# Post-norm and residual add of two feed-forwards and two mixers, re-ordered by bank and token tile, with the last store split

## What is computed

```python
u = rms_norm(x, norm_gains[layer, 0])
mix = mixer(u, ...)                               # "mix0" / "mix1"
x = x + rms_norm(mix, norm_gains[layer, 1])
u = rms_norm(x, norm_gains[layer, 2])
ff = conv_ffn(u, w_up, conv_w, conv_b, w_down)    # D_FF = 2816
x = x + rms_norm(ff, norm_gains[layer, 3])        # layer 1: this is the output
```

## Time and profile before

| | us |
|---|---|
| median of 3 executions | 1035.88 (1035.08 to 1036.29) |
| the profiled execution, its own time | 1036.02 |
| span of its profile | 1034.6 |
| TensorE matmul busy | 981.4 (95%) |
| VectorE busy | 735.9 (71%) |
| ScalarE busy | 617.1 (60%) |
| POOL busy | 40.5 (4%) |

### The profile page before, as it was taken

How to read it: one execution, slowest core, us unless ns; L and a number is a source line. 1 busy time by engine, 2 the same in 40 slices (tenths; PEclk the granted TensorE clock), 3 DMA queues, 4 the chain that set the end, 5 groups by cost and what they waited for, 6 DMA issues and landing times.

```text
span 1034.6 us, 16633 instructions
## 1 busy us (share of the span) xinstructions
PE 981.4 (95%) x6732; PEld 838.1 (81%) x6732; DVE 735.9 (71%) x1137; ACT 617.1 (60%) x1001; POOL 40.5 (4%) x37
## 2 busy tenths in 40 slices
PE   6999989999999999998999999979999979999996
PEld 5877768987778998886888888879888868888885
DVE  4866465746576778676777777776976668777776
ACT  5655664436765764576656665675447666566655
POOL 0000000000000125000000000002200000000000
PEclk9999998999999999999999999999999989999999
DMA  8733344554235432325456666635544636666551
GB/s 293 240 99 119 102 143 122 183 171 135 82 102 164 135 110 85 121 82 182 145 192 192 186 184 187 192 112 162 165 125 130 195 107 201 187 194 187 183 183 41
DMA packets 43564, 158.34 MB, mean 153 GB/s; under 512 B 4960, under 2 KB 5344, under 8 KB 43360
## 3 DMA queue, kind: packets, MB, share of 16 engines
q1 hardware_dynamic: 42480, 154.00, 47.7%
q0 software_dynamic: 576, 2.10, 0.7%
q10 hardware_dynamic: 432, 1.20, 0.3%
HBM read 156.22 MB, written 1.05 MB: 152 GB/s over the span
## 4 chain that ended last, share of the span: by engine, by line
PE 73%; DVE 12%; ACT 11%; issue 2%; DMA 2%; ACTq 0%; DVEq 0%
PE psum L393 72%; DVE w_lo L379 4%; ACT w_hi L370 2%; DVE u_lo L559 1%; ACT u_hi L548 1%; PE psum L402 1%; DMA feat<-in_norm_gains 1%; DVE scr L2736 1%; ACT normed L491 1%; DMA const<-in_table 1%; ACT scr L2726 0%; ACT normed L2606 0%; DVE x_res L2873 0%; ACT L2361 0%; DVE scr L2864 0%
## 5 line engine op out<-in xcount | busy, mean ns | idle before, releaser
L379 DVE TENSOR_TENSOR w_lo<-raw,w_hi 128x1024 fp32r<-128x1024 f32 x288 | 351.8, 1225 | 136.9 <-ACT w_hi L370 136.8
L370 ACT ACTIVATE w_hi<-raw 128x1024 fp32r<-128x1024 f32 x288 | 302.7, 1056 | 205.3 <-PE psum L393 204.9
L393 PE MATMUL psum<-u_both,w_hi 128*128 128x512 f32 x704 | 250.3, 398 | 0.6 <-DVE u_both L559 0.6
L393 PE MATMUL psum<-u_both,w_lo 128*128 128x256 f32 x704 | 197.6, 281 | 0.0
L393 PE MATMUL psum<-w_hi,u_hi 128*128 128x512 f32 x432 | 176.6, 409 | 10.7 <-DVE u_lo L559 4.1
L393 PE MATMUL psum<-w_lo,u_hi 128*128 128x512 f32 x432 | 170.6, 395 | 0.0
L393 PE MATMUL psum<-w_hi,u_lo 128*128 128x512 f32 x432 | 170.5, 395 | 0.0
L393 PEld LDWEIGHTS psum<-u_both,w_hi 128*128 128x128 f32 x704 | 132.2, 188 | 33.2 <-DVE u_both L559 0.9
L393 PEld LDWEIGHTS psum<-u_both,w_lo 128*128 128x128 f32 x704 | 132.9, 189 | 1.5
L393 PE MATMUL psum<-u_hi,w_hi 128*128 128x256 f32 x384 | 111.0, 289 | 2.2 <-DVE w_lo L379 1.8
L393 PE MATMUL psum<-u_lo,w_hi 128*128 128x256 f32 x384 | 108.6, 283 | 0.0
(11 more groups left out here) (290 smaller groups left out, 1174.9 us busy)
## 6 DMA issues: line engine op xcount, KB each, us to landing
raw<-in_pieces SPq DMA_DIRECT2D x288, 512.0 KB, 3.7
feat<-in_norm_gains POOLq DMA_DIRECT2D x4, 512.0 KB, 5.2
const<-in_table SPq DMA_DIRECT2D x1, 1240.0 KB, 7.2
x_res<-in_x SPq DMA_DIRECT2D x1, 512.0 KB, 4.9
x_res<-in_x ACTq DMA_DIRECT2D x1, 512.0 KB, 5.1
out_x<-x_res SPq DMA_DIRECT2D x1, 512.0 KB, 2.7
out_x<-x_res ACTq DMA_DIRECT2D x1, 512.0 KB, 2.8
cols<-in_cols SPq DMA_DIRECT2D x1, 380.0 KB, 4.2
```

The lines of the kernel that those rows point to most:

```text
L370: act.q.activation(w_hi[i % SPLIT][:, :], raw[i % RAW][:, :], ACT.Copy).then_inc(act.done, act.mark("hi", i))
L379: dve.q.tensor_tensor(w_lo[i % SPLIT][:, :], raw[i % RAW][:, :], w_hi[i % SPLIT][:, :].bitcast(F32), ALU.subtract).then_inc(dve.done, dve. ...
L393: return pe.q.matmul(o, lhs, rhs, start=start, stop=stop, **kw)
```

## The change

At the mixers' ends VectorE does product and add of token tile 0, then product and add of token tile 1. At the feed-forwards' ends TensorE signals every bank; ScalarE squares the banks in order and makes the root of each token tile by itself; VectorE multiplies a bank after it has been squared, joins the sums by token tile, and adds by halves, token tile 0 before the last product of token tile 1, in both layers. After feed-forward 0 TensorE turns all of token tile 0 before token tile 1. The store of token tile 1 is made in two halves of columns, the first from ACT's queue, the second from SP's. The number of products, squares and transposes stays; there is one more sum, Ln and Exp to each feed-forward, two half adds in place of each full add in layer 1, and one more DMA.

```diff
         sp.wait_ge(dve, "f1", "x", 0)
         sp.q.dma_start(out[0, 0:P, :], x_res[:, 0, :]).then_inc(out_written, 16)
-        sp.q.wait_ge(out_written, 32)
+        sp.wait_ge(dve, "f1", "x", 1)
+        sp.q.dma_start(out[0, P:2 * P, NC:D], x_res[:, 1, NC:D]).then_inc(out_written, 16)
+        sp.q.wait_ge(out_written, 48)
...
         for t in range(ST):
             dve.wait_ge(act, "mix_sq", l, 1, t)
             dve_mix_gain(l, 1, t)
-        for t in range(ST):
             dve.wait_ge(act, "rstd", name, t)
             dve.wait_ge(dve, "mix_gain", l, 1, t)
             dve.q.scalar_tensor_tensor(x_res[:, t, :], mix_gained[:, t, :], post_rstd[name][:, t:t + 1], x_res[:, t, :],
...
-            if t == 0 and j == FT - 1:
-                last.then_inc(pe.done, pe.mark("ffn", l, 0))
+                if j == FT - 1 and (t, c) != (ST - 1, 1):
+                    last.then_inc(pe.done, pe.mark("ffn", l, t, c))
...
     def act_ffn_end(l):
...
+        act_ffn_square(l, 0, 0)
+        act_ffn_square(l, 0, 1)
+        act_ffn_square(l, 1, 0)
+        act_ffn_rstd(l, 0)
+        act_ffn_square(l, 1, 1)
+        act_ffn_rstd(l, 1)
+
+    def dve_ffn_gain(l, t, c):
+        cs = slice(c * NC, (c + 1) * NC)
+        dve.wait_ge(act, "square", f"f{l}", t, c)
+        dve.q.tensor_tensor(ffn_gained[:, t, cs], ffn_out[:, t, cs], post_gain[:, cs], ALU.mult).then_inc(
+            dve.done, dve.mark("times_gain", f"f{l}", t, c))
+
+    def dve_ffn_sum(l, t):
+        for c in range(2):
+            dve.wait_ge(act, "square", f"f{l}", t, c)
+        dve.q.tensor_tensor(post_sums[f"f{l}"][:, t:t + 1], ffn_sums[:, 0, t:t + 1], ffn_sums[:, 1, t:t + 1],
+                            ALU.add).then_inc(dve.done, dve.mark("post_sum", f"f{l}", t))
+
+    def dve_ffn_add(l, t):
+        dve.wait_ge(act, "rstd", f"f{l}", t)
+        for c in range(2):
+            cs = slice(c * NC, (c + 1) * NC)
+            dve.wait_ge(dve, "times_gain", f"f{l}", t, c)
+            dve.q.scalar_tensor_tensor(x_res[:, t, cs], ffn_gained[:, t, cs], post_rstd[f"f{l}"][:, t:t + 1],
+                                       x_res[:, t, cs], ALU.mult, ALU.add).then_inc(
+                dve.done, dve.mark(f"f{l}", "x" if c else "x0", t))
...
     def dve_ffn_end(l):
...
+        dve_ffn_gain(l, 0, 0)
+        dve_ffn_sum(l, 0)
+        dve_ffn_gain(l, 0, 1)
+        dve_ffn_gain(l, 1, 0)
+        dve_ffn_add(l, 0)
+        dve_ffn_sum(l, 1)
+        dve_ffn_gain(l, 1, 1)
+        dve_ffn_add(l, 1)
...
     def pe_c():
-        for kk in range(4):
-            pe_feature("n10", x_res, kk, [(dve, "f0", "x" if kk // 2 else "x0", t) for t in range(ST)])
+        for t in range(ST):
+            for kk in range(4):
+                pe.wait_ge(dve, "times_gain", "f0", kk // 2, kk % 2)
+                pe.wait_ge(dve, "f0", "x" if kk // 2 else "x0", t)
+                for j in range(2):
+                    last = tr(psum[:, 4 + kk, (j * ST + t) * P:(j * ST + t + 1) * P],
+                              x_res[:, t, (2 * kk + j) * P:(2 * kk + j + 1) * P])
+                if t == ST - 1:
+                    last.then_inc(pe.done, pe.mark("turned", "n10", kk))
...
-        act.wait_ge(dve, "f1", "x", 1)
-        act.q.dma_start(out[0, P:2 * P, :], x_res[:, 1, :]).then_inc(out_written, 16)
+        act.wait_ge(dve, "f1", "x0", 1)
+        act.q.dma_start(out[0, P:2 * P, 0:NC], x_res[:, 1, 0:NC]).then_inc(out_written, 16)
```

More of the change, by code:

```diff
@@ L2777, in pe_down @@
         if j == FT - 1:
-            pe.also("ffn", l, 1)
+            pe.also("ffn", l, ST - 1, 1)
     def pe_ffn(l, free):
@@ L2838, in dve_ffn, with act_ffn_square @@
         dve_ffn_end(l)
-    def act_ffn_end(l):
[L2843 to L2853, removed]
+    def act_ffn_square(l, t, c):
+        act.wait_ge(pe, "ffn", l, t, c)
+        act.q.activation(normed[:, t, c * NC:(c + 1) * NC], ffn_out[:, t, c * NC:(c + 1) * NC], ACT.Square,
+                         accum_out=ffn_sums[:, c, t:t + 1]).then_inc(act.done, act.mark("square", f"f{l}", t, c))
@@ new lines, in act_ffn_rstd @@
+    def act_ffn_rstd(l, t):
+        act.wait_ge(dve, "post_sum", f"f{l}", t)
+        act_rstd(post_sums[f"f{l}"][:, t:t + 1], D, post_rstd[f"f{l}"][:, t:t + 1], f"f{l}", t)
+    def act_ffn_end(l):
+        act_ffn_square(l, 0, 0)
[9 more added lines that the diff above has]
+            dve.done, dve.mark("times_gain", f"f{l}", t, c))
@@ L2855, in dve_ffn_end @@
     def dve_ffn_end(l):
-        name = f"f{l}"
         dve.q.wait_ge(in_post_gain, 16 * (2 * l + 2))
[L2858 to L2874, removed]
+        dve_ffn_gain(l, 0, 0)
```

## The result

The changed kernel took 1031.16 us, the median of five executions (1029.93 to 1031.68), against 1036.29 (1035.08 to 1037.81) for the kernel before, run beside it: ratio 0.9948, 95% interval 0.9933 to 0.9962. A second set of five on another occasion gave 1033.19 (1031.63 to 1033.84) against 1036.18, ratio 0.9969, interval 0.9957 to 0.9981. The median of all ten is 1031.66. The forecast was 1031.4, with a range of 1029.2 to 1033.7; both medians lie in it, the second 1.8 above the forecast. Both intervals show a faster kernel; the gain is 3 to 5 us (0.3 to 0.5%), and why it isn't one number is part of what follows.

A forecast was written before the change was run, and what follows sets the result against it. The prediction took the kernel as TensorE-bound, with gains only in its waits: mixer ends 2.3, feed-forward 0 0.5, the end 1.2 and the clock 0.6 sum to 4.6, so 1036.0 − 4.6 = 1031.4 us, range 1029.2 to 1033.7.

The forecast's parts named there:

- What bounds the kernel: Whole kernel: TensorE holds 73% of the chain, so edits win only where it stands idle and waits.
- The sum: Whole kernel: gains of 2.3, 0.5, 1.2 and 0.6 add to 4.6 us, giving 1031.4 us.
- Mixer ends: Both mixer projection ends: add of tile 0 starts earlier, TensorE restarts 1.15 us sooner at each, 2.3 us together.
- the sign: Before the mixers' feature matmuls: TensorE's idle times of 3.7 and 4.0 us would show the forecast at work.
- Feed-forward 0: End of the first feed-forward: roots and adds by tile, copies limited by ScalarE's conversions; 0.5 us, bounds 0 and 0.9.
- The end: End of feed-forward 1: earlier stores, data flow sets the finish; 1.2 us gain, span ending at 1033.4.
- Rival 3: Final stores: half-row stores are slow, 2.1 us worse than the sum, 1033.5 us; chance 0.05.
- The clock: After TensorE's mixer restarts: its clock may return earlier; 0.3 us each, 0.6 together, with 0 and 1.8 as ends.
- Rival 2: Old path shadowed: conversions and store latency hide gains, leaving 2.0 to 2.8 us, 1033.2 to 1034.0; chance 0.15.
- Rival 4: After the feed-forwards: clock returns a stage late, dense quarters run at half speed, slower at 1040.6 us; chance 0.03.
- sign of being wrong: Projection after a feed-forward: granted clock below 1.0 where the dense quarters begin would show the forecast wrong.
- Rival 1: Mixer waits: clock stays up or returns at once, 2.2 us a place, up to 1027.6 us; chance 0.13.

The follow-up runs named there:

- e9: Changed kernel plus five extra constant matmuls in each mixer wait and two before and two behind feed-forward 0's transposes; 1030.01 us, ratio 0.9949.
- e4: Changed kernel with TensorE's transposes after feed-forward 0 bank by bank as before; 1031.91 us, ratio 0.9957.
- e11: Changed kernel with extra matmuls in all three waits and one weight conversion moved ahead of token tile 1's root; 1031.67 us, ratio 0.9954.
- e2: Changed kernel with the mixer ends back in the old order; 1035.25 us, ratio 0.9988.
- e3: Changed kernel with token tile 1 stored whole after its last half add; 1033.52 us, ratio 0.9977.
- e5: Changed kernel with five extra matmuls on constants in each mixer wait; 1029.68 us, ratio 0.9943.
- e6: Kernel before with five extra matmuls on constants in each mixer wait; 1034.03 us, ratio 0.9983.
- e1: Kernel before with only the mixer ends in the new order; 1034.12 us against 1036.24, ratio 0.9979.
- e7: Changed kernel with one weight conversion moved ahead of token tile 1's root in feed-forward 0; 1031.09 us, ratio 0.9955.
- e8: Changed kernel with extra matmuls in the mixer waits and one weight conversion moved ahead of token tile 1's root; 1029.63 us, ratio 0.9952.
- e10: Changed kernel with extra matmuls in the mixer waits and five ahead of feed-forward 0's transposes, done bank by bank; median 1031.13 us, ratio 0.996.

## Why the prediction was right, step by step

**What bounds the kernel** held: 4.03 of the 4.43 us lie in the waits that the earlier trace rows show and the clock behind them.

**The sum** was 0.17 off, which is luck in part: the mixer ends fell 0.66 short, and 0.40 came from stretches that were forecast at nothing, 0.27 of it between the third quarter and the end of the stall described under e9.

**Mixer ends**, forecast 2.3, measured 1.64. The mechanism was right, one term was mis-sized: I put each add 0.61 behind its product, a distance read between an add and a product whose result it didn't use. An add that waits for the product just before it starts 0.79 behind. Two such pairs a place make 0.36, and 0.32 to 0.34 are missing; TensorE's idle times are 3.96 and 4.03 where 3.7 and 4.0 were named as the sign. VectorE, which I had just free in time, is the serial resource.

**Feed-forward 0**, forecast 0.5, measured 0.66. The gate of the copies was named rightly: ScalarE's conversions, which e4 shows by an unchanged start of the copies and e11 by a moved one. The last half add ends 7.15 behind the last down group, where the sum had 7.20. The size is luck all the same: the sum let the clock fall here, and 0.66 was measured where it didn't; where it fell, 0.30 (e4), 0.03 (e2) and -0.47 (e3) are left at the third quarter.

**The end**, forecast 1.2, measured 1.23. The data flow as the measure was right (its row, 0.99 busy at 397 GB/s, stands in the earlier trace rows, not in the earlier trace rows), and e3 has its half share at 0.56 where 0.6 was worked out. Rival 3 falls: the stores of half rows ran as fast. The rule on transfer sizes in the Trainium skill (DMA: Bandwidth & Descriptors, under Bandwidth) did not decide here: by its 64 KB rate the end would have taken 2.5 us more than the sum had, and from the last down group it took 9.32 where the sum had 9.4. Its rate is for one transfer of another size; here the two halves were in flight behind another store.

**The clock**, forecast 0.6, measured 0.50 in the profiled pair. That is luck as much as reading: it is 0 and 0.5, not 0.3 twice, and at feed-forward 0, where I had put nothing, the third quarter differs by up to 1.1 us between profiles of the same code. (By the earlier trace rows it was back at 838.8 in mixer 1, 4.7 after the restart, not at 838.6.) As for its price, my 2.2 a place for a clock that doesn't fall was near (1.88 and 2.13 by e5 and e6); as the range of a single median it matters more than I gave it room for: the two medians of the same kernel are 2.03 apart.

**Rival 2** (shadowed) falls by e1, e2 and e3. **Rival 4** is real in kind, at 0.6 to 1.1 us at the third quarter (1.2 to 1.4 in e7 and e8, against e11) and not 8: five profiled executions with the new order show the dense quarters beginning at 1.2 GHz, which the prediction had named as a sign of being wrong. It didn't reverse the sign of the whole, but in e3 it did that of the stage (149.85 against 149.52). **Rival 1**, the clock up in the mixer waits, needed the extra matmuls of e5 to come true.

Open: what makes the stall in the next projection, and why it is longer with extra matmuls; why e4 is the quickest from there to mixer 1; whether the order of the transposes makes the late return more frequent.

## What to carry to other kernels

Where an engine does "product, product, add, add" on two tiles and the first add's result starts a chain on other engines, let product and add alternate, and count the own-engine wait that this exposes (0.18 us here for each pair) against it. Cut two executions at common events before comparing them; with TensorE near 95% busy, what a short wait costs depends on whether its clock falls there, and that was worth up to 2 us a wait, more than the wait's own shortening. At the end of a program put out the last bytes in a transfer of half the size as soon as each half is ready.

## What the runs showed of the hardware that was not expected

One float32 matmul call stands in the trace as two matmul records: five calls of 384 columns make the "x10" of e5, and the 16 feature calls the "x32" of the earlier trace rows. The first copy thus waits for ten calls, which is why it came behind some twenty records. The transposes are one record each.

The 5501.86 us execution of e10 was slow from its first microseconds on, long before the code that differs. The profile gives its granted clock as 1.0 and has no fall in it at all, not even behind the last matmul, so it may not have been recorded. The costliest group on the page:

```profile
L393 PE MATMUL psum<-u_both,w_hi 128*128 128x512 f32 x704 | 1193.2, 1695 | 0.0
```

1695 ns for a matmul that takes 398 elsewhere, while VectorE's `w_lo` took its usual 1.22 us: TensorE alone was slow. Neither it nor the 1099.77 of e11 (granted clock 0.845) is explained; both were kernels that keep TensorE busy in all three waits, e9 is a third one and showed nothing of the kind in six executions.
